# A mixture-of-experts kernel: the first pass's transposed rows made on TensorE, and three experts with fixed places

## What is computed

```python
def moe(h, router_w, router_b, w_gate, w_up, w_down):
    t = h.reshape(B * L, D)
    scores = jax.nn.sigmoid((t @ router_w).astype(jnp.float32))
    sel = (scores + router_b.astype(jnp.float32)).reshape(-1, N_EXPERT_GROUPS, EXPERTS_PER_GROUP)
    group_score = lax.top_k(sel, TOP_K)[0].sum(-1)
    g_best = jnp.argmax(group_score, axis=-1)
    ...
    gates = jnp.sum(jax.nn.one_hot(ids, N_EXPERTS, dtype=jnp.float32) * w[..., None], axis=1).astype(h.dtype)
    hid = jax.nn.silu(jnp.einsum('nd,edf->nef', t, w_gate)) * jnp.einsum('nd,edf->nef', t, w_up)
    y = jnp.einsum('nef,efd->nd', hid * gates[:, :, None], w_down)
```

## Time and profile before

| what | value |
|---|---|
| median of three runs | 1061.24 us |
| profiled execution, its own time | 1064.55 us |
| its span, first to last instruction | 1062.7 us |
| mean granted clock of TensorE | 0.953 of full speed |
| PE busy | 972.3 us (91%) |
| DVE, ACT, POOL busy | 406.3, 177.8, 141.6 us |
| DMA moved | 245.79 MB, 231 GB/s over the span |

### The profile page before, as it was taken

One profiled execution on the slowest core, in us unless ns is written; L12 is line 12 of the kernel. 1 busy time (PEld: TensorE's weight loads), 2 busy tenths in 40 slices (PEclk: granted clock), 3 DMA queues, 4 the chain that ended last, 5 costly groups with the idle time before them and its releaser, 6 DMA issues.

```text
span 1062.7 us, 13818 instructions
## 1 busy us (share of the span) xinstructions
PE 972.3 (91%) x5556; PEld 497.9 (47%) x5556; DVE 406.3 (38%) x908; ACT 177.8 (17%) x377; POOL 141.6 (13%) x151
## 2 busy tenths in 40 slices
PE   2799999998789996799999789999999976999997
PEld 1555445566564554443443244444555554434432
DVE  0211340114753556552333460350226474532236
ACT  4211100014661010111111151000120101111100
POOL 4100140002760000100000400010000001000003
PEclk9899999999999997699999989999999986999999
DMA  9979658975515001999999722320070008999977
GB/s 335 378 278 338 223 187 281 362 252 160 165 42 218 30 20 40 374 385 392 422 406 387 281 104 66 122 79 1 0 249 40 21 20 348 397 411 421 422 297 297
DMA packets 86693, 245.79 MB, mean 231 GB/s; under 512 B 7408, under 2 KB 22416, under 8 KB 74208
## 3 DMA queue, kind: packets, MB, share of 16 engines
q1 hardware_dynamic: 57952, 199.05, 48.7%
q0 software_dynamic: 8816, 29.04, 7.3%
q10 hardware_dynamic: 19856, 16.76, 5.1%
HBM read 216.71 MB, written 27.33 MB: 230 GB/s over the span
## 4 chain that ended last, share of the span: by engine, by line
PE 83%; DMA 7%; DVE 5%; issue 2%; ACT 2%; POOL 1%; SPq 0%; DVEq 0%; ACTq 0%; POOLq 0%
PE bank L1747 25%; PE bank L1863 17%; PE bank L1759 14%; PE bank L1877 8%; DMA ring<-in_ada_w 4%; PE bank L1703 4%; PE bank L1717 4%; PE bank L1854 3%; PE bank L2046 1%; PE bank L1773 1%; PE bank L2121 1%; DVE x_res L1238 1%; DMA uv<-h_rows,small 1%; PE bank L2038 1%; PE bank L2173 1%
## 5 line engine op out<-in xcount | busy, mean ns | idle before, releaser
L1747 PE MATMUL bank<-ring,h_feat 128*128 128x512 f32 x640 | 282.1, 598 | 3.7 <-issue 2.7
L1747 PEld LDWEIGHTS bank<-ring,h_feat 128*128 128x128 f32 x640 | 120.6, 191 | 151.3 <-issue 150.1
L1863 PE MATMUL bank<-ring,uv 128*32 128x512 f32 (+2 forms) x608 | 164.1, 609 | 1.4 <-ACT uv L969 1.4
L1759 PE MATMUL bank<-ring,h_feat 128*128 128x512 f32 x320 | 148.6, 615 | 0.0
L1863 PEld LDWEIGHTS bank<-ring,uv 128*32 128x32 f32 (+2 forms) x608 | 53.3, 136 | 82.6 <-issue 79.0
L1759 PEld LDWEIGHTS bank<-ring,h_feat 128*128 128x128 f32 x320 | 60.4, 196 | 66.6 <-issue 66.5
L1877 PE MATMUL bank<-ring,uv 128*32 128x512 f32 (+2 forms) x304 | 79.7, 595 | 1.0 <-ACT uv L984 0.6
L1467 DVE TENSOR_TENSOR uv<-uv,bank 128x256 f32<-128x256 f32 x25 | 10.5, 421 | 138.7 <-ACT uv L977 138.7
L1717 PE MATMUL bank<-ring,small 128*2 128x128 f32 x1152 | 38.9, 290 | 24.4 <-DMA ring<-in_ada_w 24.4
L859 POOL DMA_INDIRECT uv<-h_rows,small x25 | 23.7, 947 | 209.2 <-PE bank L1854 165.9
L1863 PE MATMUL bank<-h_feat,uv 128*32 128x512 f32 (+2 forms) x208 | 49.4, 594 | 0.0
(11 more groups left out here) (231 smaller groups left out, 1051.2 us busy)
## 6 DMA issues: line engine op xcount, KB each, us to landing
ring<-in_ada_w SPq DMA_DIRECT2D x16, 2048.0 KB, 14.0
ring<-in_moe_w_gate SPq DMA_DIRECT2D x20, 1024.0 KB, 12.9
ring<-in_moe_w_up SPq DMA_DIRECT2D x20, 1024.0 KB, 15.5
ring<-in_moe_w_down SPq DMA_DIRECT2D x20, 1024.0 KB, 15.3
h_tok<-in_moe_w_down SPq DMA_DIRECT2D x12, 1024.0 KB, 16.6
y_rows<-uv SPq DMA_DIRECT2D x23, 512.0 KB, 14.1
ring<-in_na_w_in SPq DMA_DIRECT2D x4, 2048.0 KB, 16.8
bz<-in_ada_w SPq DMA_DIRECT2D x4, 2048.0 KB, 12.9
```

The source lines that it names most:

```text
L1747: last = mm(jbank(key)[:, :], HT[:, cc, P * t:P * (t + 1)], w[:, cc, :], start=cc == 0, stop=cc == DC - 1)
L1759: last = mm(jbank(key)[:, :], HT[:, cc, P * t:P * (t + 1)], blk_ap(("out", layer, b))[:, cc, :], start=cc == 0, stop=cc == DC - 1)
L1863: last = mm(bank[2][32 * q:32 * (q + n), :], XT[:, b, cc, 32 * q:32 * (q + n)], w[:, :, cc, :], start=cc == 0, stop=cc == DC - 1)
```

## The change

It touches both layers alike.

- PE makes the feature-major rows of the first pass without memory: for each token tile, `first_rows` multiplies the rows in `H` (as weights, 8 slices of 128 features) by a one-hot matrix of 128 tokens by 128 places and sums the five tiles in PSUM banks 0 and 1. `place` makes this matrix per tile (`first_place`, `first_oh`). Tiles 0 to 2 stand after `indices(3)`, tiles 3 and 4 after the counts. The first gather and the first pass's transposes are gone; POOL begins with the second pass.
- Experts 0, 1 and 2 have the places 0, 1 and 2 (`FIXED = 3`), and only 13 are ranked; `QUARTERS` and `RANK_AT` are new, with 13 and 12 passes as before.
- SP issues the loads of places 1 and 2 ahead of its wait for the expert numbers; the loop over ranked places starts at 3.
- DVE's last steps of the ranking move into `rank_experts`, behind the copy of the first pass's rows. The table of tokens is copied to SBUF first (`idx_sb`), and the index of the second pass, which holds two fixed experts, is made ahead of the expert numbers. PE makes that index between the second and third chunk of the first pass's `gate_up`, and the other passes' indices after it.

```diff
@@ -39,11 +39,12 @@
...
-QUARTERS = [[4, 5, 4, 3, 3, 2, 3, 5, 3, 2, 2, 6, 3, 3, 2, 2], [4, 4, 3, 3, 2, 4, 3, 3, 2, 4, 3, 3, 2, 4, 2, 2]]
-RANK_AT = [[1, 3, 4, 5, 10, 6, 2, 7, 11, 12, 0, 8, 9, 13, 14], [0, 4, 5, 10, 1, 6, 7, 11, 2, 8, 9, 12, 3, 13, 14]]
+FIXED = 3
+QUARTERS = [[4, 3, 3, 2, 6, 2, 5, 3, 3, 3, 2, 4, 5, 3, 2, 2], [4, 3, 3, 2, 4, 3, 3, 2, 4, 4, 3, 3, 2, 4, 2, 2]]
+RANK_AT = [[8, 0, 9, 1, 4, 5, 6, 10, 3, 2, 7, 11, 12], [8, 0, 4, 5, 9, 1, 2, 6, 7, 10, 3, 11, 12]]
 PASSES = [sum(q) // 4 for q in QUARTERS]
 NPASS = max(PASSES)
-RANKED = E - 1
+RANKED = E - FIXED
 MAXOV = 12
...
@@ -140,7 +141,7 @@
...
     def gathers_before(self, s):
-        return len(range(s, self.before.passes, 3)) if self.before else 0
+        return len(range(s or 3, self.before.passes, 3)) if self.before else 0
...
@@ -404,6 +405,7 @@
...
+        first_oh = PS[:, 1024:1664].rearrange("p (t n) -> p t n", t=TT)
         last_router_rows = UV[:, 3584:4096].rearrange("p (c n) -> p c n", c=4)
...
@@ -422,6 +424,7 @@
...
         gs, gtied, goff, one1, one2 = routing(4), routing(4), routing(4), routing(1), routing(1)
+        first_place, idx_sb = routing(1), routing(2 * E)
         prod2, pos2 = routing(2 * E).rearrange("p (k e) -> p k e", k=2), routing(2)
@@ -449,7 +452,7 @@
...
         idx_all, late_sums = bank[7][:, 0:2 * E], bank[7][:, 96:96 + NTILE + MAXOV]
-        idx_low, idx_high = idx_all[:, 0:E], idx_all[0:PLACES - P, E:2 * E]
+        idx_low, idx_high = idx_sb[:, 0:E], idx_sb[0:PLACES - P, E:2 * E]
         idx_pass = bank[7][:, 64:64 + NPASS]
@@ -665,7 +669,7 @@
...
             def ranked_expert(p):
-                return sp.value_load(ids_i[0:1, p - 1:p], min_val=0, max_val=E - 1)
+                return sp.value_load(ids_i[0:1, p - FIXED:p - FIXED + 1], min_val=0, max_val=E - 1)
...
@@ -692,8 +696,11 @@
...
                         wait_mod(sp, 1, g)
+                for p in range(1, FIXED):
+                    load_gate_up(layer, p, p)
+                    load_down(layer, p, p)
                 sp.wait_ge(ids_ready, 2 * layer + 1)
-                for p in range(1, WSLOTS):
+                for p in range(FIXED, WSLOTS):
                     ex = ranked_expert(p)
...
@@ -850,7 +857,6 @@
...
                     pool.dma_start(h2_rows[layer][P * t:P * (t + 1), :], H[:, t, :]).then_inc(h2_stored, 16)
-                pool.wait_ge(idx_ready, 3 * layer + 1)
                 pool.wait_ge(h2_stored, 16 * TT * (layer + 1))
...
@@ -860,9 +866,9 @@
...
-                for e in range(passes):
-                    if e in (1, 3):
-                        pool.wait_ge(idx_ready, 3 * layer + (2 if e == 1 else 3))
+                for e in range(1, passes):
+                    if e <= 2:
+                        pool.wait_ge(idx_ready, 3 * layer + 1 + e)
                     if e >= 3:
...
@@ -1292,6 +1298,9 @@
...
                     dve.wait_ge(pos_done, (TT + 1) * layer + t + 1)
+                    link(nc.vector.tensor_scalar(first_place, pos[:, t, 0:1], 1.0, both[:, 0:1], ALU.add, ALU.mult))
+                    nc.vector.tensor_scalar(first_oh[:, t, :], iota[:, 0:P], 1.0, first_place, ALU.add, ALU.is_equal)\
+                        .then_inc(first_oh_ready, 1)
                     tt(prod2, picks[:, t, :, :], row(pos[:, t, :], 2), ALU.mult)
...
@@ -1337,24 +1346,30 @@
...
                 dve.wait_ge(pos_done, (TT + 1) * (layer + 1))
-                link(nc.vector.scalar_tensor_tensor(rank_key, cnt[:, 1:E], float(E), rank16[:, 1:E], ALU.mult, ALU.add))
+                link(nc.vector.scalar_tensor_tensor(rank_key, cnt[:, FIXED:E], float(E), rank16[:, FIXED:E], ALU.mult,
+                                                    ALU.add))
                 tt(rank_oh, row(rank_key, RANKED), bc(rank_key, RANKED), ALU.is_gt)
                 red(rank_of, rank_oh, ALU.add)
+
+            def rank_experts(layer):
+
                 dve.wait_ge(idx_mm, (TT + 2) * layer + TT)
-                nc.vector.tensor_copy(idx_i[:, 0:1], idx_low[:, 0:1]).then_inc(idx_ready, 1)
-
+                nc.vector.tensor_copy(idx_sb, idx_all).then_inc(idx_ready, 1)
                 tt(rank_oh, bc(rank_of, RANKED), row(ranks, RANKED), ALU.is_equal)
+                pass_indices(layer, 0, 1, 2)
                 oh_by_rank = rank_oh.rearrange("p e r -> p r e")
...
                 nc.vector.tensor_copy(ids_i, ids).then_inc(ids_ready, 1)
-                tt(by_rank, oh_by_rank, row(idx_low[:, 1:E], RANKED), ALU.mult)
+                dve.wait_ge(idx_ready, 3 * layer + 1)
+                tt(by_rank, oh_by_rank, row(idx_low[:, FIXED:E], RANKED), ALU.mult)
                 red(tok_low, by_rank, ALU.add)
...
                 link(nc.vector.tensor_tensor(by_rank[high], oh_by_rank[high],
-                                             idx_high[:, 1:E].unsqueeze(1).to_broadcast([PLACES - P, RANKED, RANKED]),
+                                             idx_high[:, FIXED:E].unsqueeze(1).to_broadcast([PLACES - P, RANKED, RANKED]),
                                              ALU.mult))
                 nc.vector.tensor_reduce(tok_high[high], by_rank[high], AX, ALU.add).then_inc(ids_ready, 1)
+                nc.vector.tensor_copy(idx_i[:, 0:1], idx_low[:, 0:1])
...
@@ -1373,10 +1388,14 @@
...
                 nc.vector.memset(start[:, 0:1], 0.0)
-                link(nc.vector.memset(cap[:, 0:1], 32.0 * QUARTERS[layer][0]))
+                for p in range(FIXED):
+                    if p:
+                        nc.vector.memset(start[:, p:p + 1], float(PLANS[layer].first_row[p]))
+                    ins = nc.vector.memset(cap[:, p:p + 1], 32.0 * QUARTERS[layer][p])
+                link(ins)
                 for out, table in ((start, first_row), (cap, room)):
                     tt(by_rank, rank_oh, row(table, RANKED), ALU.mult)
-                    red(out[:, 1:E], by_rank, ALU.add)
+                    red(out[:, FIXED:E], by_rank, ALU.add)
                 tt(excess, cnt, cap, ALU.subtract)
...
@@ -1466,7 +1485,7 @@
...
                     if e == 0:
-                        pass_indices(layer, 1, 3, NPASS)
+                        pass_indices(layer, 1, 2, NPASS)
                         read_xt(1, base + 2)
...
@@ -1480,7 +1499,7 @@
...
                 read_xt(0, base + 1)
-                pass_indices(layer, 0, 1, 3)
+                rank_experts(layer)
                 route_weights(layer)
...
@@ -1781,6 +1800,14 @@
...
+                def first_rows(t):
+                    pe.wait_ge(first_oh_ready, TT * layer + t + 1)
+                    pe.wait_ge(h2_ready, TT * layer + t + 1)
+                    for cc in range(DC):
+                        last = mm(bank[cc // 4][:, P * (cc % 4):P * (cc % 4) + P], H[:, t, cc::DC], first_oh[:, t, :],
+                                  start=t == 0 and cc % 4 == 0, stop=t == TT - 1 and cc % 4 == 3)
+                    return last
+
                 def indices(t):
...
@@ -1830,23 +1857,33 @@
...
                 indices(TT - 2)
+                for h in range(2):
+                    wait_read(pe, ("o", layer, TT - 1, h))
+                    wait_read(pe, ("r", layer, TT - 1, h))
+                for t in range(TT - 2):
+                    first_rows(t)
                 positions(TT - 1)
...
                 mm(cnt, ones, both, start=False, stop=True).then_inc(pos_done, 1)
+                for t in range(TT - 2, TT):
+                    last = first_rows(t)
+                last.then_inc(xt_mm, 1)
                 indices(TT - 1)
             def pass_indices(layer, part, passes):
-                pe.wait_ge(ids_ready, 2 * (layer + 1))
                 pe.wait_ge(idx_ready, 3 * layer + 1 + part)
+                if part:
+                    pe.wait_ge(ids_ready, 2 * (layer + 1))
                 for e in passes:
...
                         if k < 4:
-                            last = mm(out, ident[:, 32 * k:32 * (k + n)], tok_low[:, p - 1:p], start=True, stop=True)
+                            toks = idx_low[:, p:p + 1] if p < FIXED else tok_low[:, p - FIXED:p - FIXED + 1]
+                            last = mm(out, ident[:, 32 * k:32 * (k + n)], toks, start=True, stop=True)
                         else:
                             last = mm(out, ident[0:PLACES - P, 32 * (k - 4):32 * (k - 4 + n)],
-                                      tok_high[0:PLACES - P, p - 1:p], start=True, stop=True)
+                                      tok_high[0:PLACES - P, p - FIXED:p - FIXED + 1], start=True, stop=True)
                 last.then_inc(idx_mm, 1)
...
@@ -1856,8 +1893,8 @@
...
-            def gate_up(b, tiles, slot):
-                for cc in range(DC):
+            def gate_up(b, tiles, slot, chunks=range(DC)):
+                for cc in chunks:
                     for q, n, p, _ in tiles:
...
@@ -1913,9 +1950,12 @@
...
                     gate_up_weights(e)
-                    gate_up(b, plan.tiles[e], turn).then_inc(gu_mm, 1)
                     if e == 0:
```

(19 more changed lines are left out.)

## The result

The changed kernel takes 1062.40 us (median of 20 runs, 1060.12 to 1065.95), the kernel before 1059.61 in runs beside them (20 runs, 1052.01 to 1063.51): a ratio of 1.0037, 95% interval 1.0022 to 1.0052. It is slower by a little, where the forecast was 1.2% faster. The profiled execution of after took 1060.31 us, its span is 1058.5.

What follows compares the result with a forecast made beforehand. TensorE, busy 91% of the span, was taken as the bound, its first pass late and mostly at half clock. Terms -3.8 - 4.6 - 2.2 - 2.2 - 0.3 = -13.1 us gave 1048.1 in the median, range 1042.5 to 1056.

Steps and rivals of the forecast that it cites:

- PE, first_rows: TensorE's matmuls for the first pass's rows: 8.4 us for tiles 0 to 2, 4.0 for tiles 3 and 4.
- Start of the first pass: First gate and up matmuls at 429.0 us in layer 0, 884.4 in layer 1: gains of 3.8 and 4.6.
- place(): Two added VectorE instructions per tile, 0.5 us for the pair, uncovered for tile 3, so indices(3) ends 0.5 later.
- Positions and counts, indices(4): Small TensorE matmuls behind the first three tiles and behind the last two: 8 instructions, 1.0 us each.
- Positions queued behind: The last tile's positions wait in TensorE's queue behind first_rows, putting 3 us into that tile's routing.
- To the second pass: Stretch from first to second pass's matmuls: TensorE and VectorE about level, gather not late, 2.2 us won per layer.
- G + 12.3: VectorE's path to the second pass ends 12.3 us after G, the first pass's new start; TensorE's path takes 12.2.
- Loads: Six early weight DMAs for places 1 and 2, 6.3 MB, in by about 425 us; no gain or loss counted.
- The second pass: Its matmuls' duration: no change from 9.12 us in layer 0, 8.05 in layer 1; bounds -2.1 and -1.1, or +0.9 each.
- The first one: Rival: clock stays down through first_rows, 0.248 us per instruction, 1071 us in all; loses from mean 0.235; chance 0.09.
- the late gather: Rival: the second pass's gather takes 9.1 us, giving back the 2.2 us per layer: 1052.3 us, chance 0.12.
- an estimate of 0.25 per instruction: By the skill's transpose factor, a layer's 40 first_rows matmuls would take about 20 us at full clock, not 9.9.

Runs made afterwards that it cites:

- the late-load run: The changed kernel with the six loads of places 1 and 2 put back behind the wait for the expert numbers: 1086.55 us, ratio 1.0245.
- the run with positions first: The changed kernel with positions and counts of the last tile put ahead of all of first_rows: 1073.27 us, ratio 1.0135.

## Why the prediction was wrong

The step that failed is one term, *PE, first_rows*: "the nearest row is L2031, 16 of them in 1.98 us, 0.124 each at full clock". The row agrees in operation, size and type and not in the layout of the weights, and the forecast put no bound on that. By it 48 instructions took 8.4 us and 32 took 4.0; measured are 11.49 and 7.72, together 6.8 us more per layer. At 1.00 the change pays 0.24 where the forecast had 0.124. (Its half-clock price, 0.248 as twice the full one, is near the 0.24 that the change pays there, but not for that reason: contiguous weights measured 0.21 at 0.50.) Nothing else of size is off:

- *Start of the first pass.* Forecast 20.3 [20.8] us after the out projection, measured 27.5 [27.5]: 7.2 and 6.7 late, of which 6.8 is `first_rows`; in layer 0 a further 0.5 went before indices(3) ended, which came 6.4 after the out projection and not 5.9.
- *place().* 0.5 us for the pair; the two start 0.26 and 0.20 apart from what follows, 0.46.
- *Positions and counts, indices(4).* 1.0 each; 0.80 and 1.14.
- *Positions queued behind.* 3 us were counted, 6.9 were measured (416.6 to 423.45), for the most part by the same term (3.1 us).
- *To the second pass.* G + 12.3; measured 12.7 [12.1]. Neither the second gather nor weights ended a wait of PE there.
- *Loads.* In by about 425, 16.3 us after the out projection; they leave at 405.6, the DMA engines move 340 GB/s in the stretch that ends at 422.2, 224 in the next and 5 in the one from 425.6, so they are in by 425.6 at the latest, up to 20 us after the out projection. Later by up to 4 us, and still no wait hangs on them; the late-load run shows what the cover is worth.
- *The second pass.* 7.67 [8.18] against 9.12 [8.05], inside the bounds. (The passes of 64 instructions hold pieces of 32 columns of two experts by `QUARTERS`, not four experts; the terms taken from them stay.)

The misses of the two stages sum to 7.2 + 6.7 + 0.4 - 0.2 = 14.1 us, next to the distance between forecast and result, 1062.4 - 1048.1 = 14.3. That closeness is luck. Between the two profiled executions the forecast missed by 1060.31 - 1051.4 = 8.9, since outside the two stages the trace of after is 5.6 us shorter than that of before. Between the medians it missed by 15.9, 13.1 us won in the forecast and 2.8 lost in the runs, since the median of before is 1061.24 in three runs and 1059.61 in twenty.

With the cause taken away the first pass starts 19.7 [19.8] us behind the out projection, where 20.3 [20.8] were forecast, and the second 12.1 [12.1] later, where 12.3 were: the other terms held to within 1.0 us to the first pass and 0.2 behind it. That the kernel then takes 1048.12 us, the forecast's 1048.1, is luck again in part: it is 11.0 under its own runs of before (1059.11), not 13.1.

*The rivals.* The first one gave the right price, 0.248, and its break-even, 0.235 per instruction, is where the kernel ended: at 0.24 it should lose 0.4 us per layer, and it stands at +1.7 and -0.3. But its cause was wrong. It laid the price on a clock that stays down, with everything behind it slow too, hence 1071; the clock was 1.00 in the middle of `first_rows` and the price still 0.24, and half clock alone, with contiguous weights, would have cost 0.21, under the break-even. A price worked out for one cause held for another. (A slip in the late gather: two layers that give back 2.2 us each make 1052.5, not 1052.3.)

The Trainium skill ("TensorE: Matmul & The Clock Gate", Terms) states that transpose mode is four times faster for FP32, from which the prediction made an estimate of 0.25 per instruction. The traces agree with that factor only for weights at step 8: there 16 instructions take 7.72 / 2 = 3.86 us and eight transposes 0.96 (from 455.85 in after), a factor of 4.0. With contiguous weights 16 instructions of 0.115 are 1.83 us and a transpose group 0.91 to 1.04 at full clock, a factor of 1.8 to 2.0. So it was the layout that made the price, and not the mode.

*What stays open.* The two profiled executions explain +1.4 us up to the second passes; the interval of the ratio says 2.3 to 5.5. The rest was not found in a stage. The profile of after was 2.1 us under the median of its kernel and that of before 4.9 above its own (1064.55 and 1059.61), and of the 5.6 us by which they differ outside the stages 3.1 lie ahead of the end of layer 0's out projection. Nor does one trace hold a stage closely: in the kernel before with reordered rows layer 1 takes 37.8 us to the second pass, in that of before 39.9, with a gather of 4.29 us against 5.93. Why a weight load is slow at steps 4 and 8 and not at 2 is not shown by any run.

## What to carry to other kernels

A price is taken from a row that agrees in the access pattern too, not only in shape and type; where the trace has no such row, both ends stand in the range. Before rows are handed to TensorE as weights, let the engine that writes them put the values of one weight tile side by side: here that costs VectorE 1.5 us per tile, mostly under other work, and turns +0.4% into -1.1%. When a queue is filled ahead of a step that others wait for, look for what waits next: here VectorE's reordered write.

## What the runs showed of the hardware

- At full clock a 128x128 f32 weight load takes 192 ns from contiguous values, about 196 at step 2, 308 to 335 at steps 4 and 8. At step 8 the load sets the pace, 0.24 us per instruction at 1.2 as at 2.4 GHz; contiguous it is 0.115 at 2.4 GHz and 0.21 at 1.2, where the load takes 333 ns. Step 8 cost the gathered rows' transposes next to nothing (0.95 against 0.90 us for eight at full clock, 1.99 against 1.98 at half).
- The granted clock fell to 0.50 while `first_rows` ran without a gap (880.60 to 884.00 in after, PE and PEld busy 3.40 of 3.40, DMA idle), after 1.00 in the three stretches ahead of it. So a PE that the profile shows as busy can still lose its clock; why it fell was not settled. The step alone does not do it: in the run with positions first the same loads kept 1.00 from 425.6 us to their end. With contiguous weights the clock stayed at 1.00 to the end of `first_rows` once it had come back.
- VectorE writing and reading 1024 values in another order (inner step 8) takes 1.99 and 2.02 us in place of 1.28 and 1.22.
